# Reordering ScalarE and VectorE work in the gated-recurrence stage of a two-block float32 kernel

## The reference, cut to what matters

```python
def rglru_mixer(h, w_in, conv_w, conv_b, w_a, b_a, w_x, b_x, lam, w_out):
    gate, xr = jnp.split(h @ w_in, 2, axis=-1)
    gate = jax.nn.gelu(gate)
    xc = conv_b + xpad[:, 0:S] * conv_w[0]            # 4 taps along the tokens
    ...
    r = jax.nn.sigmoid(... xb @ w_a + b_a)            # 4 diagonal blocks of 256
    i = jax.nn.sigmoid(... xb @ w_x + b_x)
    log_a = (-RG_C * r) * jax.nn.softplus(-lam)
    a = jnp.exp(log_a)
    u = jnp.sqrt(-jnp.expm1(2.0 * log_a)) * (i * xc)
    hs = associative_scan(a, u)                       # h[t] = a[t] h[t-1] + u[t]
    return (hs * gate) @ w_out
```

## Time and profile before

| what | value |
|---|---|
| median of 3 runs | 901.79 us (901.32 to 910.28) |
| profiled execution, its own time | 901.79 us |
| its span in the trace | 900.1 us |
| outside the span | 1.7 us |
| TensorE busy | 866.2 us, 96% of the span |
| VectorE, ScalarE, GpSimd busy | 692.5, 464.3, 171.9 us |
| mean granted TensorE clock | 0.992 of full speed |

### The profile page before, as it was taken

The page is one execution under the profiler, slowest core; times in us unless marked ns, Lnnn a source line. Parts: engine busy times, 40 slices in busy tenths (PEclk is TensorE's granted clock), DMA queues, the critical chain, the costliest instruction groups (busy, mean ns, idle before and its releaser), DMA issues.

```text
span 900.1 us, 17916 instructions
## 1 busy us (share of the span) xinstructions
PE 866.2 (96%) x6992; PEld 823.4 (91%) x6992; DVE 692.5 (77%) x1066; ACT 464.3 (52%) x673; POOL 171.9 (19%) x188
## 2 busy tenths in 40 slices
PE   7999999999999997899999999999999999999998
PEld 6998899999999985599999999989899898999998
DVE  5897788889977688667766677678668998997793
ACT  7782355564443356645555444354367546646641
POOL 6222300014432000021000122242203322013000
PEclk9999999999999997999999999999999999999999
DMA  9754576678998442044666666555535544545542
GB/s 347 244 196 145 190 253 225 230 267 255 275 287 208 151 137 94 1 129 176 194 206 198 200 191 201 191 181 189 186 129 177 165 159 147 178 150 187 178 151 94
DMA packets 46961, 167.87 MB, mean 187 GB/s; under 512 B 5776, under 2 KB 5920, under 8 KB 46640
## 3 DMA queue, kind: packets, MB, share of 16 engines
q1 hardware_dynamic: 40896, 146.82, 49.0%
q0 software_dynamic: 5856, 20.00, 7.7%
q10 hardware_dynamic: 144, 0.15, 0.1%
HBM read 165.50 MB, written 1.44 MB: 185 GB/s over the span
## 4 chain that ended last, share of the span: by engine, by line
PE 73%; DVE 14%; ACT 5%; issue 5%; DMA 2%; POOL 1%; DVEq 0%; ACTq 0%; SPq 0%; POOLq 0%
PE bank L556 20%; PE bank L558 19%; PE bank L557 19%; PE bank L623 5%; DVE wlo L1313 4%; ACT whi L963 2%; DVE ada_prod L1488 2%; PE bank L641 2%; PE bank L783 1%; DVE xl L1332 1%; DVE tq L1519 1%; DMA ada_raw<-ada_w 1%; PE bank L878 1%; PE bank L888 1%; PE bank L837 1%
## 5 line engine op out<-in xcount | busy, mean ns | idle before, releaser
L1313 DVE TENSOR_TENSOR wlo<-raw,whi 128x1024 fp32r<-128x1024 f32 x260 | 317.8, 1256 | 92.8 <-ACT whi L963 91.7
L556 PE MATMUL bank<-xh,whi 128*128 128x256 f32 x1328 | 374.6, 282 | 7.0 <-DVE xl L1332 2.1
L558 PE MATMUL bank<-xh,wlo 128*128 128x256 f32 x1328 | 369.3, 278 | 0.0
L557 PE MATMUL bank<-xl,whi 128*128 128x256 f32 x1328 | 369.3, 278 | 0.0
L963 ACT ACTIVATE whi<-raw 128x1024 fp32r<-128x1024 f32 x260 | 265.8, 1052 | 145.6 <-PE bank L558 121.4
L556 PEld LDWEIGHTS bank<-xh,whi 128*128 128x128 f32 x1328 | 249.1, 188 | 18.2 <-issue 8.6
L557 PEld LDWEIGHTS bank<-xl,whi 128*128 128x128 f32 x1328 | 249.3, 188 | 0.2
L558 PEld LDWEIGHTS bank<-xh,wlo 128*128 128x128 f32 x1328 | 249.2, 188 | 0.0
L556 PE MATMUL bank<-hhi,whi 128*128 128x256 f32 x512 | 142.3, 278 | 3.0 <-DVE wlo L1313 3.0
L558 PE MATMUL bank<-hhi,wlo 128*128 128x256 f32 x512 | 142.0, 277 | 0.0
L557 PE MATMUL bank<-hlo,whi 128*128 128x256 f32 x512 | 141.9, 277 | 0.0
(11 more groups left out here) (278 smaller groups left out, 1076.3 us busy)
## 6 DMA issues: line engine op xcount, KB each, us to landing
raw<-weights SPq DMA_DIRECT2D x260, 512.0 KB, 4.5
ada_raw<-ada_w POOLq DMA_DIRECT2D x24, 512.0 KB, 5.0
plain<-plain_w SPq DMA_DIRECT2D x16, 512.0 KB, 6.7
relB<-rel_scratch POOLq DMA_DIRECT2D x8, 256.0 KB, 8.2
bl<-rpb_in POOLq DMA_DIRECT2D x32, 64.0 KB, 3.6
x<-x_in SPq DMA_DIRECT2D x4, 256.0 KB, 5.9
cond<-cond_in POOLq DMA_DIRECT2D x1, 1024.0 KB, 7.4
cx<-ctx_in POOLq DMA_DIRECT2D x1, 1024.0 KB, 8.0
```

The source lines that it names most:

```text
L556: mmul(dst, hi, rh, start=start, stop=False)
L557: mmul(dst, hi, rlo, start=False, stop=False)
L558: return mmul(dst, lo, rh, start=False, stop=stop)
L1313: V_.tensor_tensor(wlo[:, sl], raw[:, sl], whi[:, sl].bitcast(F32), ALU.subtract)\
```

## The change

Only the order within ScalarE's and VectorE's programs is changed. The rows of TensorE, GpSimd and SyncE are the same, in the same order. On ScalarE, the `lamt` work goes ahead of `root(0)` and `split(0, 1)`, and all four `rg_root` stand together after `split(1, 1)`. On VectorE, the two chunks of `split(0, 0)` and the `lamt` and `qg8` work go ahead of `rstd(0)`; the copy of the relative-position table goes behind `conv(1)`; `one_minus_a2(0)` and `(1)` go behind `split(1, 0)`; `scan(0)` and `scan(1)` go behind `split(1, 1)`; and the last scans, `y` and `empty_gate(3)` are woven differently.

```diff
@@ ScalarE
             split(0, 0)
-            root(0)
-            split(0, 1)
             ch.link(A(lamt[:, 0], col("lam", 0, 8), ACT.Abs))
             ch.link(A(lamt[:, 1], lamt[:, 0], ACT.Exp, scale=-1.0))
             A(lamt[:, 2], lamt[:, 1], ACT.Ln, bias=ones[:, 0:1]).then_inc(S_["lam_parts"], 1)
             A(lamt[:, 3], col("lam", 0, 8), ACT.Relu, scale=-1.0).then_inc(S_["lam_parts"], 1)
+            root(0)
+            split(0, 1)
...
             split(1, 0)
-            rg_root(0)
-            rg_root(1)
             sigmoids(1)
             tanhs(1)
             decays(1)
             split(1, 1)
-            rg_root(2)
-            rg_root(3)
+            for n in range(4):
+                rg_root(n)
@@ VectorE
-            split_chunk(0, 0)
+            split(0, 0)
+            V_.tensor_scalar(qg8[:], col("q_g"), 64.0 ** -0.5, None, ALU.mult)
+            dve.wait_ge(S_["lam_parts"], 2)
+            ch.link(V_.tensor_tensor(lamt[:, 1], lamt[:, 2], lamt[:, 3], ALU.add))
+            V_.tensor_scalar(lamt[:, 4], lamt[:, 1], RG_C, None, ALU.mult).then_inc(S_["lam_ready"], 1)
+            V_.tensor_scalar(lamt[:, 5], lamt[:, 1], -RG_C, None, ALU.mult).then_inc(S_["lam_ready"], 1)
...
             conv(0)
-            split_chunk(0, 1)
+            empty_xr(1)
+            conv(1)
             dve.wait_ge(S_["rel_psum"], 1)
             V_.tensor_copy(relt[:], bank[4][0:H1, 0:RLEN]).then_inc(S_["rel_table"], 1)
-            empty_xr(1)
-            conv(1)
...
             conv(3)
-            one_minus_a2(0)
-            one_minus_a2(1)
             split(0, 3)
             empty_gate(0)
             split(1, 0)
-            scan(0)
-            scan(1)
+            one_minus_a2(0)
+            one_minus_a2(1)
             empty_gate(1)
             one_minus_a2(2)
             one_minus_a2(3)
             split(1, 1)
+            scan(0)
+            scan(1)
             empty_gate(2)
+            y(0)
             scan(2)
-            y(0)
             y(1)
             scan(3)
+            empty_gate(3)
             y(2)
-            empty_gate(3)
             y(3)
             split(1, 2)
```

## The result

| what | before | after |
|---|---|---|
| median of 20 runs | 907.37 us (900.58 to 910.28) | 912.87 us (905.29 to 916.27) |
| profiled execution, its own time | 901.79 us | 914.05 us |
| its span in the trace | 900.1 us | 912.4 us |

The ratio, from the fast runs on record (one of the changed kernel, at 922.25 us, is left out as slow), is 1.0067, with a 95% interval from 1.0044 to 1.0091: the change makes the kernel slower by 0.7%. The two medians in the table are 5.5 us apart, 0.6%. The absolute number that was forecast (907.6, range 902.7 to 910.0) misses 912.87, because the kernel before has itself a median of 907.37 over 20 runs, and not the 901.79 of the first three. The forecast difference was 5.85 us.

A forecast was written before the change was run, and what follows sets the result against it. TensorE, busy 96% of the span, was taken to bound the kernel. The sum was 901.79 + 3.95 (waits up to rec_out's k = 6) + 1.9 (one clock fall) = 907.6 us, range 902.7 to 910.

The forecast's parts named there:

- Step 1, the root: ScalarE's start: lamt work ahead of the root moves it from 17.89 to about 20.04 us.
- Step 2, the table copy: VectorE's table copy ends at 31.19 instead of 26.07, so TensorE waits 0.9 us before block_gates(0).
- Step 3: Through the end of gate: everything 0.9 us later, VectorE idle some 6 us, split(1, 1) still in time.
- Step 4, the tail: VectorE's last scans and y: TensorE waits 1.2 and 2.4 us in rec_out; k = 6 is 3.95 us late in all.
- Step 5, the clock: TensorE's clock falls once to 0.50 around rec_out's waits, costing 1.9 us.
- The base of the sum: Whole kernel: the profiled execution's 901.79 us, taken as equal to the median, without correction.
- The clock holding: Rival: TensorE's clock stays up through both rec_out waits, 905.7 us; chance 0.2.
- The tail hidden: Rival: VectorE gives y before rec_out on TensorE wants it, only the table-copy wait remains, 902.7 us; chance 0.09.
- the gain of 0.5 us: Rival: y(3) comes in time, the wait before rec_out's k = 6 vanishes, 901.3 us; chance 0.04.
- a clock that stays low for over 10 us: Rival: in rec_out, low clock for 10.6 us costs 5.3, giving 911.0 us; chance 0.12, shared with another stage's fall.
- A fall in another stage: Rival: another stage's clock falls too; put at 911.0 us with the long low clock, joint chance 0.12.

The follow-up runs named there:

- The head alone: Kernel before with only the change's early part: lamt work ahead of the root, split(0, 0) and lamt ahead of the reciprocal, table copy behind conv(1); ratio 1.0001.
- the copy kept early: Kernel before with the new early order on ScalarE and VectorE, but the table copy between conv(0) and empty_xr(1); ratio 0.9995.
- the filled run: Changed kernel plus unread matmuls on TensorE, 2 ahead of rec_out's k = 2 and 4 ahead of k = 4; ratio 1.006.
- a swap: Kernel before with empty_gate(3) moved ahead of y(2) on VectorE; ratio 0.997 (0.9932 to 1.0008).
- the tail alone: Kernel before with only the change's later part: new VectorE order of one_minus_a2, scan, y and empty_gate(3), four rg_root together on ScalarE; ratio 1.0055.
- the run with the roots grouped: Kernel before with only the four rg_root together behind split(1, 1) on ScalarE, VectorE's order unchanged; ratio 1.0106.

## Why the prediction was right or wrong

- **Step 1, the root: right.** Forecast 20.04, found 19.93. The Exp ran without a table load. The instruction behind a load started 1.29 us after it again (16.93, and 18.22 for the Ln), as in the kernel before.
- **Step 2, the table copy: right.** Forecast end 31.19, found 30.55 + 0.54 = 31.09; `block_gates(0)` at 31.15 against 31.25. The head alone cost 0.90 us, and with the copy kept early nothing.
- **Step 3: right.** `split(1, 1)` was in time (no wait for a chunk), the hole 6.80 us.
- **Step 4, the tail: right.** Forecast `scan(0)` 67.4, `y(2)` 77.9, k = 4 at 78.65; found 67.41, 77.95, 78.68. The mixer's delay of 5.43 less 1.46 of clock is 3.97, against the 3.95 of the sum. The two waits were 1.10 and 2.10 us, a little under the stated 1.2 and 2.4.
- **Step 5, the clock: right in mechanism, a little off in size.** The clock fell once; it cost 1.46 us against the 1.9 taken and the 0.9 to 2.4 allowed. Part of the low time lay in the wait, as the lower end supposed. In the repeat of the changed kernel it also lasted 3.4 us, but fell all within the work: 27.85 us for the 120 rows, 1.68 us. Two other runs had it low for twice as long, 28.95 and 28.76 us for the 120 rows, 2.8 and 2.6 us, above the upper end. So the price of a fall was known only to about a factor of two.
- **The base of the sum: wrong.** "The profiled execution's own time equals the median, so no correction is needed." That median came from three runs, two of them in the quick group, and the profile was one of the quick executions. The row of 910.28 among the three was the other group, not an outlier. Over 20 runs the base is 907.37, and 907.37 + 5.85 = 913.2 against 912.87. The difference was about right (5.85, against 5.50 between the medians, 6.4 and 6.7 between like groups, and 5.43 and 5.72 at the mixer's end in the two profiles of the changed kernel). Its base and so the range were not: the range had no term for a second level 7 us higher, in a stage that the change does not touch. Against the lower group alone the forecast stands: 907.6, and that group's median is 908.00.
- **The rivals.** The clock holding (905.7) takes TensorE kept busy, as the filled run shows. The tail hidden, and the gain of 0.5 us, failed on VectorE's order as stated; the gain itself is real, by a swap. The last, a clock that stays low for over 10 us, did not occur; 6.8 was the longest in the mixer. A fall in another stage, which was put with it, did occur in the first MLP, in executions of either kernel.

## What to carry to other kernels

An idle stretch of a helper engine is worth something only if work that is due later is already in it: moving 4 us of scans out of a hole and in front of the work that TensorE waits for cost some 3 us of waits and 1.5 or more of clock, while saving a table load gained nothing. Before a sum is put on a median, look at whether the runs fall into groups, and which group the profiled execution belongs to. When two profiles differ by more than the changed stage does, compare like events after it before looking for a cause in the change, and take a second profile of the same kernel.

## What the runs showed of the hardware

Three things were not expected. TensorE has two steady paces here at the same granted clock: a unit of 48 matmuls of 128x256 (each with its weights) takes 5.44 or 5.65 us. Each profiled execution kept one of the two through the second MLP, whatever pace other stages had, and the timed runs of one instruction order lie in two groups some 6 to 7 us apart, as the pace of the second MLP would make them. The same standing of TensorE for 1.1 and 2.1 us was followed by 3.4 us of low clock in two executions (the changed kernel's) and by 6.8 us in another (the tail alone). And where nothing ahead of it had changed, the first L641 row moved between 29.90 and 31.20 us from one execution to the next, with the length of the first plain stage (8.61 us in the third execution of before, 9.96 in the run with the roots grouped).
